# Two-layer, two-block network on one core: converting the first weight tile in two halves and moving the sums of squares behind the second tile's conversion

## The reference, cut to what matters

```python
def rms_norm(x, g):
    xf = x.astype(jnp.float32)
    y = xf * lax.rsqrt(jnp.mean(xf * xf, axis=-1, keepdims=True) + EPS)
    return (y * g.astype(jnp.float32)).astype(x.dtype)
...
    u = rms_norm(h, g_mix_pre)
    (gq, gk, gv, gg, ra_f, ra_b, aq, ak, av, gate_a, gate_b) = jnp.split(u @ w_in, offsets, axis=-1)
```

## Time and profile before

| | before |
|---|---|
| median of 3 runs | 2329.11 us (2327.55 to 2329.76) |
| the profiled execution's own time | 2325.64 us |
| its span in the trace | 2323.8 us |
| PE busy in the span | 2283.4 us, 98% |
| DVE busy | 1578.6 us, 68% |
| ACT busy | 1317.6 us, 57% |
| mean granted TensorE clock | 0.996 of full speed |

### The profile page before, as it was taken

One profiled execution on the slowest core, in us unless ns is written; L12 is line 12 of the kernel. 1 busy time (PEld: TensorE's weight loads), 2 busy tenths in 40 slices (PEclk: granted clock), 3 DMA queues, 4 the chain that ended last, 5 costly groups with the idle time before them and its releaser, 6 DMA issues.

```text
span 2323.8 us, 31048 instructions
## 1 busy us (share of the span) xinstructions
PE 2283.4 (98%) x13016; PEld 2001.0 (86%) x13016; DVE 1578.6 (68%) x1799; ACT 1317.6 (57%) x1783; POOL 38.8 (2%) x66
## 2 busy tenths in 40 slices
PE   8999999999999999899999999999999999999998
PEld 8888888888998888788898888888888898888886
DVE  6866766479766775657576766774676578666655
ACT  5675555466655655545447755554654558555554
POOL 1000000010000000010000000000100000000000
PEclk9999999999999999999999999999999999999999
DMA  8516565565345655565564455555665655455553
GB/s 262 181 56 191 188 200 182 186 207 186 109 136 191 200 182 190 181 196 182 182 190 164 127 181 190 183 197 182 192 206 179 200 161 165 143 184 181 182 191 117
DMA packets 323131, 412.57 MB, mean 178 GB/s; under 512 B 9360, under 2 KB 245008, under 8 KB 322992
## 3 DMA queue, kind: packets, MB, share of 16 engines
q1 hardware_dynamic: 318160, 395.47, 52.3%
q0 software_dynamic: 4544, 14.12, 1.9%
q10 hardware_dynamic: 288, 0.99, 0.1%
HBM read 409.51 MB, written 1.05 MB: 177 GB/s over the span
## 4 chain that ended last, share of the span: by engine, by line
PE 79%; DVE 11%; ACT 8%; issue 1%; DMA 1%; SPq 0%; DVEq 0%; ACTq 0%
PE banks L592 23%; PE banks L595 12%; PE banks L655 9%; PE banks L656 9%; PE banks L657 9%; DVE lo L1668 5%; ACT hi L1124 4%; PE banks L578 3%; PE banks L580 3%; PE banks L579 3%; DMA raw<-in_w_in 1%; PE banks L706 1%; DVE mg L1814 1%; PE banks L839 0%; PE banks L816 0%
## 5 line engine op out<-in xcount | busy, mean ns | idle before, releaser
L1668 DVE TENSOR_TENSOR lo<-raw,hi 128x2048 fp32r<-128x2048 f32 (+1 forms) x384 | 860.8, 2245 | 571.1 <-ACT hi L1124 571.0
L1124 ACT ACTIVATE hi<-raw 128x2048 fp32r<-128x2048 f32 (+1 forms) x384 | 717.0, 1872 | 218.8 <-DMA raw<-in_ffn_w_out 85.2
L592 PE MATMUL banks<-x_in,hi 128*128 128x512 f32 x2304 | 577.7, 393 | 1.3 <-issue 1.2
L592 PEld LDWEIGHTS banks<-x_in,hi 128*128 128x128 f32 x2304 | 414.7, 189 | 75.7 <-issue 1.5
L595 PEld LDWEIGHTS banks<-x_in,lo 128*128 128x128 f32 x2304 | 314.5, 191 | 22.3
L595 PE MATMUL banks<-x_in,lo 128*128 128x256 f32 x2304 | 321.4, 283 | 0.0
L578 PE MATMUL banks<-x_in,hi 128*128 128x256 f32 x752 | 215.6, 287 | 0.0
L580 PE MATMUL banks<-x_in,lo 128*128 128x256 f32 x752 | 213.2, 283 | 0.0
L579 PE MATMUL banks<-x_in,hi 128*128 128x256 f32 x752 | 213.1, 283 | 0.0
L655 PE MATMUL banks<-hi,x_hid 128*128 128x512 f32 x528 | 206.3, 391 | 0.0
L656 PE MATMUL banks<-lo,x_hid 128*128 128x512 f32 x528 | 205.8, 390 | 0.0
(11 more groups left out here) (334 smaller groups left out, 3109.8 us busy)
## 6 DMA issues: line engine op xcount, KB each, us to landing
raw<-in_w_in SPq DMA_DIRECT2D x108, 1024.0 KB, 5.2
raw<-in_ffn_w_in SPq DMA_DIRECT2D x88, 1024.0 KB, 5.1
raw<-in_w_ffn_in SPq DMA_DIRECT2D x44, 1024.0 KB, 5.1
raw<-in_ffn_w_out SPq DMA_DIRECT2D x40, 1024.0 KB, 5.1
raw<-in_w_ffn_out SPq DMA_DIRECT2D x20, 1024.0 KB, 5.1
raw<-in_w_o_gla SPq DMA_DIRECT2D x8, 1024.0 KB, 5.2
raw<-in_w_o_attn SPq DMA_DIRECT2D x8, 1024.0 KB, 5.1
raw<-in_w_out SPq DMA_DIRECT2D x8, 1024.0 KB, 5.0
```

The costliest lines, as they stand in the source:

```text
L592: pe.matmul(to, wh[:, k, cut], x[:, k, :, :].rearrange("p n s -> p (n s)"), start=(k == 0), stop=(k == KD - 1), skip_group_check=True)
L1124: act_fn(high, of, ACT.Copy).then_inc(hi_done.up(), 1)
L1668: tt(rest, of, parts(tile, hi)[0].bitcast(F32), ALU.subtract).then_inc(lo_done.up(), 1)
```

## The change

The first weight tile is converted in two halves of 128 x 1024 (each two of the tile's four blocks of the contraction) on ACT and on DVE. Two new semaphores, `front_hi` and `front_lo`, say that the first half is done; `hi_done` and `lo_done` of tile 0 now follow the second half. On ACT the order becomes: first half high, first turned high part, second half high, second turned high part, tile 1 high, the sums of squares of both groups of token rows, the third and fourth turned high parts. On DVE: gain of the first rows, both remainder halves, the first two turned remainders, tile 1's remainder, gain of the second rows, the last two turned remainders. PE starts the first product on `front_lo` and waits for `lo_done` in the middle of its first eight matmuls. SP's and POOL's code is unchanged.

```diff
+    "front_hi": (0, 0), "front_lo": (0, 0),
...
+        front_hi, front_lo = signal("front_hi"), signal("front_lo")
...
-            def rows_a(tile, x, to, t, first, last, late=None, turn=None):
+            def rows_a(tile, x, to, t, first, last, late=None, turn=None, back=None):
...
                     for k in range(tile.kc):
+                        if back and k == tile.kc // 2:
+                            pe.wait_ge(*back)
                         xh = x[:, tile.k0 + k, 0, lanes]
...
-            def rows_in_turn(tiles, x, banks, start, first_turns, third, fourth):
+            def rows_in_turn(tiles, x, banks, start, first_turns, third, fourth, front=None):
...
+                        back = lo_done.at(tile.index + 1) if front and t == i == 0 else None
                         if t == 0:
-                            pe.wait_ge(*lo_done.at(tile.index + 1))
+                            pe.wait_ge(*(front if back else lo_done.at(tile.index + 1)))
...
-                                    turns[2 * t + i])
+                                    turns[2 * t + i], back)
...
-            rows_in_turn(BY1["gva"], x_in, (0, 1), 0, (), *high_turns[2:])
+            rows_in_turn(BY1["gva"], x_in, (0, 1), 0, (), *high_turns[2:], front_lo.at(1))
...
+            act.wait_ge(*landed(TILES1[0]))
+            for i, done in enumerate((front_hi, hi_done)):
+                cut = slice(i * TILE // 2, (i + 1) * TILE // 2)
+                act_fn(hi[0][:, cut], raw[0][:, cut], ACT.Copy).then_inc(done.up(), 1)
+                turned_high(x_in, *high_turns[i])
+            made[0] = 1
+            pump(1)
             for t in range(T):
                 act.wait_ge(*x_loaded[t].at(1))
                 norm_tile(t)
-                pump(t)
-                turned_high(x_in, *high_turns[2 * t])
-                turned_high(x_in, *high_turns[2 * t + 1])
+            turned_high(x_in, *high_turns[2])
+            turned_high(x_in, *high_turns[3])
...
                 for n in range(2):
                     with_gain(0, t, n)
-                pump(t)
-                turned_low(x_in, *high_turns[2 * t])
-                turned_low(x_in, *high_turns[2 * t + 1])
+                if t == 0:
+                    for i, (high, done) in enumerate(((front_hi, front_lo), (hi_done, lo_done))):
+                        cut = slice(i * TILE // 2, (i + 1) * TILE // 2)
+                        dve.wait_ge(*high.at(1))
+                        tt(lo[0][:, cut], raw[0][:, cut], hi[0][:, cut].bitcast(F32), ALU.subtract).then_inc(done.up(), 1)
+                    turned_low(x_in, *high_turns[0])
+                    turned_low(x_in, *high_turns[1])
+                    made[0] = 1
+                    pump(1)
+            turned_low(x_in, *high_turns[2])
+            turned_low(x_in, *high_turns[3])
```

More of the change, by code:

```diff
@@ L41 @@
 TOTALS = {
-    "const_in": (0, 0), "first_row": (0, 0), "ident_in": (0, 0), "up_in": (3, 0), "rope_in": (6, 0), "par_in": (0, 8), "pt_in": (1, 1), "row_in0": (1, 1), "row_in1": (2, 2),
+    "const_in": (0, 0), "front_hi": (0, 0), "front_lo": (0, 0), "first_row": (0, 0), "ident_in": (0, 0), "up_in": (3, 0), "rope_in": (6, 0), "par_in": (0, 8), "pt_in": (1, 1), "row_in0": (1, 1), "row_in1": (2, 2),
     "row_in2": (1, 1), "row_in3": (1, 1), "row_used": (5, 5), "layer_done": (1, 1), "zeroed": (1, 1),
```

## The result

The changed kernel takes 2334.12 us (median of 19 runs, 2331.24 to 2336.24) against 2328.89 us (19 runs, 2325.86 to 2331.11) for the kernel before: a ratio of 1.002, with a 95% interval of 1.0013 to 1.0027. It is slower by 5.2 us. The forecast was 2329.0, with a range that ended at 2331.0, and 0.03 for slower by over 0.2%. It was wrong.

A forecast was written before the change was run, and what follows sets the result against it. PE, busy 98% of the span, was taken as the bound. Start -0.63 plus fifth tile's load +0.5 gave -0.1 us: 2325.64 to 2325.5 profiled, 2329.11 - 0.1 = 2329.0 us on the median's scale; range 2326.2 to 2331.0.

The forecast's parts named there:

- Halves worth nothing: Start, tile 0: PE's idle transposes last until 13.67, so converting in halves gains 0 to 0.14 us, lost again before tile 1.
- Tile 1's load as the limit: Start, ACT: the load lands at 13.57, so PE starts tile 1 only 0.63 us sooner, where ACT's order alone gives 1.5.
- The sums of squares and the second gain behind, without cost: Start, ACT and DVE behind tile 1: both finish before PE's third turn needs them, ACT 0.8 us ahead; no cost.
- POOL's shift: POOL's queue: the fourth `xn_ready` comes 3.0 us later, so its first transfer moves from 16.92 to 19.9.
- the term x: Fifth tile's load: what POOL's shifted traffic adds to its 7.40 us, taken as +0.5 us.
- the upper bound: Fifth tile's load: all 0.45 MB that q0 moved from 23.3 to 26.9 goes ahead of it, adding 1.3 us.
- The lower end: Fifth tile's load: 0.26 MB of rotation tables on q0 may move out behind its end, changing it by -0.7 us.
- the slower case: Rival, chance 0.2: POOL's transfers hold up the fifth tile's load from 0.63 us on; at 1.3 us added, 0.7 us slower, 2329.8.
- The bound of "5.3 us more on a load of 7.4": Fifth tile's load: the extra time said to be needed before the kernel is 0.2% (4.7 us) slower.
- The rule that spoke against the change: DMA engines go round queues packet by packet, so POOL's 4 KB packets take the larger part; the sum would be +0.7 us.
- behind L895 nothing new is met: After the alpha matmuls' wait: PE has 32.15 us of work in the 32.80 us from 37.30 to 70.10; later waits stay.
- its own signs of being wrong: Tile 1's load not lasting until 13.6, L895 waiting over a microsecond, or the difference at 70 us not that at the end.

The follow-up runs named there:

- experiment 6: The changed kernel with the sums of squares and tile 1 back in the earlier order on ACT and DVE, so only the halves remain: 2329.08 us, ratio 1.0003.
- experiment 7: The changed kernel with POOL started at tile 1's high part and SP's load of tile 1 ahead of the second token rows: 2327.04 us, ratio 0.9991.
- experiment 10: The changed kernel with POOL's small gain rows and rotation tables sent only after the fifth tile's load has landed: 2329.47 us, ratio 1.0001.
- experiment 3: The changed kernel with 26 idle transposes on PE just before its wait for the alpha matmuls: 2328.41 us, ratio 1.0002.
- experiment 1: The changed kernel with POOL starting its transfers at tile 1's high part, not after the gain on all token rows: 2328.74 us, ratio 1.0.
- experiment 4: The changed kernel with the second token rows' gain ahead of tile 1's remainder on DVE: 2329.31 us, ratio 0.9999.

## Why the prediction was wrong, by its own steps

**The start was right.** Halves worth nothing (13.67 said, 13.65 measured; experiment 6). Tile 1's load as the limit (13.57 said, high part at 13.53 measured; experiment 7). PE's start of tile 1 (17.88 said, 17.83 measured). The sums of squares and the second gain behind, without cost: the third turned high part waited for PE and not for ACT (ACT had 1.12 us of idleness ahead of it). POOL's shift (19.9 said, 19.74 measured), and the fifth tile's load issued at 24.65 (24.59).

**The step that failed first is the term x.** The mechanism and its place were right, and it was given as a rival; the size was off. "All of it ahead of the load at the 0.36 MB per us" gave 1.3 us as the upper bound, and 0.5 was taken; it measured 3.07. Two things were wrong in it. The stretch, 23.3 to 26.9, was the one before the load's own packets began, and was taken as if they would begin no later; they began 3.2 us after the issue and not 1.7 (experiment 10). The traffic that a shift moves into the load's life is that of the stretch before its issue: from 21.7 to 25.28 q0 moved 0.70 MB in before, and in the changed kernel q0 moved 0.78 MB more during the load than before (1.21 against 0.43). At 0.36 MB per us that is 2.2 us. And the price by bytes was too low, because the earlier trace rows itself had 0.45 MB at 59.4% of the engines in 3.6 us, which is 2.1 us of engine time and not 1.3. The lower end, tables that move out behind the load, did not happen: POOL issued the second pair of tables at 27.97 and 29.78 against 26.61 and 27.27 before, well inside the load.

**The step that failed second was not in the sum at all.** The prediction priced a wait of PE at its length. It said the slower case decides at x = 0.63 and costs x - 0.63; at the measured x that is 2.4 us. The clock then added 3.47 + 1.2 = 4.7 us in the traces, against an execution of before that had no fall there, and experiment 3 puts the removal of the clock's falls, with the load as late, at 5.7 us between medians. Between the medians of the change and of before the clock's part is smaller, by estimate 5.2 - 2.4 = 2.8 us, because before's usual execution has some fall of its own. The bound of "5.3 us more on a load of 7.4" for a loss of 0.2% was wrong for that reason: 3.1 us more were enough. The profile before held the warning: a wait of PE for `rat` that any delay of the load would lengthen, three runs that all lay 2 to 4 us above the profiled one, and, in the same trace, the 10.2 us at half clock at PE's 6.27 us wait for `xn`, which the prediction did not read.

**The rule that spoke against the change**, of the Trainium skill (DMA: Bandwidth & Descriptors, section "Queues, rings and completion order"), gave x at its upper end, 1.3 us, and so the better sign; the measured 3.07 lies beyond both readings. The case does not test the rule itself: packets were 1499 to 493 in the load's time, but the trace does not show when each queue had packets waiting.

**The likelihoods.** The slower rival had 0.2, with the right place and the wrong price; "behind L895 nothing new is met" was wrong, since PE met a slower clock there. Two of its own signs of being wrong came: L895 waited over a microsecond (3.3), and the difference near 70 us, 7.1, was 0.5 short of the one at the end. The range was not the sum of its terms: 2329.11 - 1.5 - 1.6 is 2326.0 and 2329.11 + 0.7 + 0.7 is 2330.5, where 2326.2 and 2331.0 were given; the measured 2334.12 is outside either.

## What to carry to other kernels

When an edit sets a signal later, follow it into every queue that waits for it, and price the transfers that it pushes onto a needed load by the engine time of the stretch before that load's issue, not by their bytes. A wait of PE is not worth its length only: here 3.1 us more of waiting cost 4.7 us on top through the clock, against an execution without a fall, and 26 idle transposes in the same place took that back. Compare the granted clock of the runs before calling a difference of a few us a gain or a loss: the profiled execution of before had a mean clock of 0.996, which 26 of 108 reach. Where a start is bound by a load, the order of the loads (experiment 7) gives what the order of the conversions cannot.

## What the runs showed of the hardware that was not expected

After 3.3 us of idleness PE ran at half clock for 10 us (39.5 to 49.7) although it was busy from 39.7 on. The clock also fell behind 16 matmuls of 32 rows with a wait of 0.27 us ahead (experiment 1, 40.5 to 43.9 us) and with none (experiment 6, and experiment 4 in layer 1), in some traces and not in others. The time at half clock did not follow the length of the wait (10.2 us behind 1.5, 6.8 behind 3.0). The mean granted clock of the 108 runs of before goes with their time: 4.7 us lie between the medians of the upper 26 and the lower 32, of the 7 us by which these runs differ. The fifth tile's load of 1 MB took between 7.0 and 10.5 us, by what POOL's queue did beside it.
